# The experts of a transformer stack in steps of 512 hidden channels instead of 256, with the next expert's rows gathered early

## The reference

```python
D_MODEL, SEQ, D_FF_3, N_EXPERTS, TOP_K = 1024, 256, 3584, 8, 2

def swiglu(x, wg, wu, wd):
    return (jax.nn.silu(x @ wg) * (x @ wu)) @ wd

def moe_swiglu(h, w_router, wg, wu, wd):
    xt = h.reshape(-1, d)
    logits = (xt @ w_router).astype(jnp.float32)
    top_v, top_i = lax.top_k(logits, TOP_K)
    gates = jax.nn.softmax(top_v, axis=-1)
    comb = jnp.sum(jax.nn.one_hot(top_i, N_EXPERTS) * gates[..., None], axis=1)
    y = jnp.zeros_like(xt)
    for e in range(N_EXPERTS):
        y = y + comb[:, e:e + 1] * swiglu(xt, wg[e], wu[e], wd[e])
    return y.reshape(bsz, s, d)
```

## Time and profile before

| what | value |
|---|---|
| median of 3 executions | 2552.34 us (2552.05 to 2553.14) |
| profiled execution, its own time | 2553.99 us |
| its span (first to last instruction) | 2552.1 us |
| expert stage: first to last scaling of gathered rows (L1825, 9 times) | 1522.4 to 2532.1 us, 126.2 us per expert |
| PE busy | 2396.1 us, 94% |
| DVE busy | 1965.9 us, 77% |
| ACT busy | 1442.5 us, 57% |
| DMA | 651.79 MB, mean 255 GB/s |

### The profile page before, as it was taken

The page is one execution under the profiler, slowest core; times in us unless marked ns, Lnnn a source line. Parts: engine busy times, 40 slices in busy tenths (PEclk is TensorE's granted clock), DMA queues, the critical chain, the costliest instruction groups (busy, mean ns, idle before and its releaser), DMA issues.

```text
span 2552.1 us, 32705 instructions
## 1 busy us (share of the span) xinstructions
PE 2396.1 (94%) x11965; PEld 2001.3 (78%) x11965; DVE 1965.9 (77%) x1889; ACT 1442.5 (57%) x1418; POOL 17.6 (1%) x33
## 2 busy tenths in 40 slices
PE   4996999998999899799999969999999999999997
PEld 4865788867788798797887968888888888888886
DVE  6888778687687656675445748898989888888897
ACT  2553433546443454464434527777777777777775
POOL 0000000000000000000000000000000000000000
PEclk8997999999999899899999979999999999999998
DMA  8358699534598445455555429999999999999995
GB/s 326 124 173 297 226 317 321 187 121 164 167 329 300 145 163 187 131 170 173 188 183 165 165 83 331 361 340 350 350 340 359 333 366 334 366 334 366 331 368 180
DMA packets 435139, 651.79 MB, mean 255 GB/s; under 512 B 20688, under 2 KB 324432, under 8 KB 435040
## 3 DMA queue, kind: packets, MB, share of 16 engines
q1 hardware_dynamic: 432880, 643.59, 74.0%
q0 software_dynamic: 2160, 6.85, 0.8%
HBM read 649.32 MB, written 1.05 MB: 255 GB/s over the span
## 4 chain that ended last, share of the span: by engine, by line
PE 84%; DVE 9%; ACT 3%; issue 3%; DMA 1%; SPq 0%; DVEq 0%; POOL 0%; ACTq 0%
PE pair L1894 25%; PE pair L1896 25%; PE pair L1895 25%; DVE rest L1079 2%; PE pair L1929 2%; PE tb L2107 2%; DVE aw L1417 1%; ACT head L677 1%; DVE aw L1098 1%; PE pair L2017 1%; PE tb L1972 1%; DMA x<-in_x 1%; ACT aw L706 1%; DVE hT L1200 0%; DVE gat L1825 0%
## 5 line engine op out<-in xcount | busy, mean ns | idle before, releaser
L1079 DVE TENSOR_TENSOR rest<-raw,head 128x2048 fp32r<-128x2048 f32 x546 | 1249.2, 2292 | 296.2 <-ACT head L677 276.4
L677 ACT ACTIVATE head<-raw 128x2048 fp32r<-128x2048 f32 x546 | 1043.2, 1912 | 308.4 <-PE pair L1896 284.9
L1894 PE MATMUL pair<-head,hTh 128*128 128x512 f32 x1864 | 749.4, 402 | 21.2 <-DVE qkv L1509 6.8
L1896 PE MATMUL pair<-head,hTl 128*128 128x512 f32 x1864 | 731.5, 392 | 0.0
L1895 PE MATMUL pair<-rest,hTh 128*128 128x512 f32 x1864 | 730.6, 392 | 0.0
L1894 PEld LDWEIGHTS pair<-head,hTh 128*128 128x128 f32 x1864 | 352.5, 189 | 100.7 <-issue 16.3
L1896 PEld LDWEIGHTS pair<-head,hTl 128*128 128x128 f32 x1864 | 352.0, 189 | 75.0
L1895 PEld LDWEIGHTS pair<-rest,hTh 128*128 128x128 f32 x1864 | 353.0, 189 | 69.3 <-issue 1.5
L1894 PE MATMUL pair<-head,aTh 128*128 128x512 f32 x776 | 307.1, 396 | 2.6 <-issue 2.6
L1895 PE MATMUL pair<-rest,aTh 128*128 128x512 f32 x776 | 303.8, 392 | 0.0
L1896 PE MATMUL pair<-head,aTl 128*128 128x512 f32 x776 | 303.7, 391 | 0.0
(11 more groups left out here) (312 smaller groups left out, 1706.9 us busy)
## 6 DMA issues: line engine op xcount, KB each, us to landing
raw<-in_moe_w_gate SPq DMA_DIRECT2D x224, 512.0 KB, 6.0
raw<-in_moe_w_up SPq DMA_DIRECT2D x224, 512.0 KB, 7.1
raw<-in_moe_w_down SPq DMA_DIRECT2D x224, 512.0 KB, 6.7
raw<-in_w_in SPq DMA_DIRECT2D x152, 512.0 KB, 4.7
raw<-in_ada_w SPq DMA_DIRECT2D x96, 512.0 KB, 5.8
raw<-in_w_ffn_in SPq DMA_DIRECT2D x88, 512.0 KB, 5.5
raw<-in_w_ffn_out SPq DMA_DIRECT2D x44, 512.0 KB, 5.5
raw<-in_w_out SPq DMA_DIRECT2D x40, 512.0 KB, 4.8
```

Of the source, the lines that this page charges most:

```text
L677: act.activation(head[:, c.split, :], raw[:, c.raw, :], ACT.Copy).then_inc(heads_done, 1)
L1079: dve.tensor_tensor(rest[:, c.split, :], raw[:, c.raw, :], head[:, c.split, :].bitcast(F32), ALU.subtract).then_inc(rests_done, 1)
L1894: pe.matmul(out_, lh, rh, start=start, stop=False, skip_group_check=True)
L1896: return pe.matmul(out_, ll, rh, start=False, stop=stop, skip_group_check=True)
```

## The change

An expert's hidden width is taken in 7 steps of 512 channels. The chunks of a step are now six: gate (two halves of the input channels), up (two halves), down (two halves of the 512 hidden channels). A gate or up chunk holds rows of 512 floats of one matrix, where before it held rows of 256 of two. Silu, product and the turned halves work on 512 columns, and the four transposes of a step stand together. Chunk count per expert (42), matmuls and bytes are as before.

At the boundary: the gather for the next expert stands behind step 0 of the present one, `xe` is made there (`gathered_out`), and it is split within the last step (`gathered_head`, `gathered_rest`). TensorE's end of an expert is the last transposes (`turn_wide`), the last down (now two chunks, 24 matmuls, in the order first 512 columns of both, then the second), the next expert's first gate chunk (`first_gate`), and the scatter. The next round then begins at the wait for `weights_ready`. Since `first_gate` does not count its chunk as used, the transposes of `ptok` do. `pslot` has memory of its own. ScalarE and VectorE put the splits of the next expert's first two chunks around `y_head` and `y_rest`.

The dense feed-forwards only lose unused parameters of their helper functions. The diff, cut to the expert part:

```diff
     STEPS3 = F3 // FB
-    PER = 3 * STEPS3
+    EB = 512
+    STEPSE = F3 // EB
+    PER = 6 * STEPSE
...
+        pslot = sb("pslot", [P, T, P], F32R)
...
             def load_expert(it, e):
-                def gu(k, s, r):
-                    cols = slice(s * FB, (s + 1) * FB)
+                def wide(k, w, s, r):
                     c = At(MOE0 + k, it, PER)
-                    load(c.place, c.placed(-RAW), landed[c.raw], [(slice(0, 1024), eg[:, bass.ds(e * KD + 4 * r, 4), cols]),
-                                                                  (slice(1024, 2048), eu[:, bass.ds(e * KD + 4 * r, 4), cols])])
-
-                def dn(k, s):
+                    cols = slice(s * EB, (s + 1) * EB)
+                    load(c.place, c.placed(-RAW), landed[c.raw], [(slice(h * 2 * EB, (h + 1) * 2 * EB), w[:, bass.ds(e * KD + 4 * r + 2 * h, 2), cols])
+                                                                  for h in range(2)])
+
+                def dn(k, s, r):
                     c = At(MOE0 + k, it, PER)
-                    load(c.place, c.placed(-RAW), landed[c.raw], [(slice(0, D), ed[:, bass.ds(e * KF + 2 * s, 1), :]),
-                                                                  (slice(D, 2 * D), ed[:, bass.ds(e * KF + 2 * s + 1, 1), :])])
-                gu(0, 0, 0)
-                gu(1, 0, 1)
-                for s in range(STEPS3 - 1):
-                    gu(2 + 3 * s, s + 1, 0)
-                    gu(3 + 3 * s, s + 1, 1)
-                    dn(4 + 3 * s, s)
-                dn(PER - 1, STEPS3 - 1)
+                    load(c.place, c.placed(-RAW), landed[c.raw], [(slice(h * D, (h + 1) * D), ed[:, bass.ds(e * KF + 4 * s + 2 * r + h, 1), :])
+                                                                  for h in range(2)])
+
+                def gate_and_up(k, s):
+                    wide(k, eg, s, 0)
+                    wide(k + 1, eg, s, 1)
+                    wide(k + 2, eu, s, 0)
+                    wide(k + 3, eu, s, 1)
+
+                def down(k, s):
+                    dn(k, s, 0)
+                    dn(k + 1, s, 1)
+                gate_and_up(0, 0)
+                for s in range(STEPSE - 1):
+                    gate_and_up(4 + 6 * s, s + 1)
+                    down(8 + 6 * s, s)
+                down(PER - 2, STEPSE - 1)
 
...
+            def silu_wide(c, s):
+
+                act.wait_ge(chunk_used, c.count())
+                act.activation(sg_e, EXPERT_BANKS[0][:, 0, :], ACT.Silu).then_inc(sem("silu_ready"), 1)
+
+            def expert_step(c, s):
+
+                make_head(c.next(2))
+                make_head(c.next(3))
+                turned_head(s)
+                make_head(c.next(4))
+                silu_wide(c.next(1), s + 1)
+                for d in (5, 6, 7):
+                    make_head(c.next(d))
...
             def expert(it, window):
-                s0 = it * STEPS3 + STEP0[3]
+                s0 = it * STEPSE + STEP0[3]
                 at = At(MOE0, it, PER)
                 make_head(at.next(2))
-                make_head(at.next(3))
                 act.wait_ge(sem("picks_turned"), it + 1)
                 act.activation(slot_weight, tb[1][:, 256:257], ACT.Copy)
-                act.activation(pslot, tb[1][:, 0:256].rearrange("p (t n) -> p t n", t=T), ACT.Copy).then_inc(sem("slots_ready"), 1)
-                silu_gate(at.next(1), s0, 1, 0, EXPERT_BANKS)
-                for s in range(STEPS3 - 1):
-                    ffn_step(at.next(2 + 3 * s), s0 + s, 1, (s + 1) % 2, EXPERT_BANKS)
-                turned_head(s0 + (STEPS3 - 1), 1)
-                make_head(at.next(PER + 1))
+                act.activation(pslot[:, :, :], tb[1][:, 0:256].rearrange("p (t n) -> p t n", t=T), ACT.Copy).then_inc(sem("slots_ready"), 1)
+                make_head(at.next(3))
+                make_head(at.next(4))
+                silu_wide(at.next(1), s0)
+                make_head(at.next(5))
+                for s in range(STEPSE - 2):
+                    expert_step(at.next(4 + 6 * s), s0 + s)
+                c = at.next(4 + 6 * (STEPSE - 2))
+                make_head(c.next(2))
+                make_head(c.next(3))
+                turned_head(s0 + (STEPSE - 2))
+                make_head(c.next(4))
+                silu_wide(c.next(1), s0 + (STEPSE - 1))
+                make_head(c.next(5))
+                make_head(c.next(6))
+                act.wait_ge(chunk_used, c.next(3).count())
+                gathered_head(it + (window + 2))
+                make_head(c.next(7))
+                turned_head(s0 + (STEPSE - 1))
+                make_head(at.next(PER))
                 act.wait_ge(sem("slots_ready"), it + 1)
                 act.wait_ge(sem("y_half"), it + 1)
                 y_head(0)
-                gathered_head(it + (window + 2))
                 act.wait_ge(chunk_used, at.next(PER - 1).count())
                 y_head(1)
+                make_head(at.next(PER + 1))
...
+
+            def gated_wide(c, s):
+                dve.wait_ge(sem("silu_ready"), s + 1)
+                dve.wait_ge(chunk_used, c.count())
+                dve.tensor_tensor(act_e, sg_e, EXPERT_BANKS[0][:, 1, :], ALU.mult).then_inc(act_ready, 1)
+
+            def expert_step(c, s):
                 make_rest(c.next(2))
-                turned_rest(s, nt)
                 make_rest(c.next(3))
-                gated_hidden(s + 1, nt, b, banks)
+                turned_rest(s)
                 make_rest(c.next(4))
+                make_rest(c.next(5))
+                gated_wide(c.next(3), s + 1)
+                make_rest(c.next(6))
+                make_rest(c.next(7))
...
-            def gathered_rest(count, between=None):
+            def gathered_out(count):
 
                 dve.wait_ge(sem("gather_done"), count)
                 dve.tensor_tensor(xe, pair[2][:, :, :].rearrange("p b (k s) -> p (b k) s", s=P),
                                   over(col8("norm_ffn_3", 1), [P, KD, P], 2), ALU.mult).then_inc(sem("gathered"), 1)
-                if between:
-                    between()
+
+            def gathered_rest(count):
+
                 dve.wait_ge(sem("xe_head"), count)
                 dve.tensor_tensor(hTl[:, :, 0:P], xe, hTh[:, :, 0:P].bitcast(F32), ALU.subtract).then_inc(sem("xe_rest"), 1)
...
             def expert(it, e, window):
-                s0 = it * STEPS3 + STEP0[3]
+                s0 = it * STEPSE + STEP0[3]
                 for t in range(T):
                     ins = dve.tensor_scalar(token_weight[:, t:t + 1], ones[:, 0:1], comb[:, t, bass.ds(e, 1)], None, ALU.mult)
                 ins.then_inc(sem("weights_ready"), 1)
                 dve.wait_ge(sem("picks_turned"), it + 1)
                 pick(lambda c: sm[:, bass.ds(e + (c + 1), 1)])
                 at = At(MOE0, it, PER)
-                make_rest(at.next(2))
-                make_rest(at.next(3))
-                gated_hidden(s0, 1, 0, EXPERT_BANKS)
-                for s in range(STEPS3 - 1):
-                    ffn_step(at.next(2 + 3 * s), s0 + s, 1, (s + 1) % 2, EXPERT_BANKS)
-                turned_rest(s0 + (STEPS3 - 1), 1)
+                for d in (2, 3, 4, 5):
+                    make_rest(at.next(d))
+                gated_wide(at.next(3), s0)
+                for s in range(STEPSE - 2):
+                    expert_step(at.next(4 + 6 * s), s0 + s)
+                    if s == 0:
+                        gathered_out(it + (window + 2))
+                c = at.next(4 + 6 * (STEPSE - 2))
+                make_rest(c.next(2))
+                make_rest(c.next(3))
+                turned_rest(s0 + (STEPSE - 2))
+                make_rest(c.next(4))
+                make_rest(c.next(5))
+                gated_wide(c.next(3), s0 + (STEPSE - 1))
+                make_rest(c.next(6))
+                gathered_rest(it + (window + 2))
+                make_rest(c.next(7))
+                turned_rest(s0 + (STEPSE - 1))
+                make_rest(at.next(PER))
+                y_rest(it, 0)
+                y_rest(it, 1)
                 make_rest(at.next(PER + 1))
-                gathered_rest(it + (window + 2), lambda: y_rest(it, 0))
-                y_rest(it, 1)
                 for t in range(T):
                     dve.wait_ge(sem("scattered"), it * 2 + (t + 1))
                     dve.tensor_tensor(x[:, t, :], x[:, t, :], pair[2 - t][:, :, :].rearrange("p b n -> p (b n)"),
                                       ALU.add).then_inc(sem("scatter_added"), 1)
 
...
+            def wide(c, bank_, r, used=True):
+
+                pe.wait_ge(rests_done, c.placed())
+                for k in range(4):
+                    wcols = slice(k * EB, (k + 1) * EB)
+                    ins = three(bank_, hTh[:, 4 * r + k, 0:P], hTl[:, 4 * r + k, 0:P], head[:, c.split, wcols], rest[:, c.split, wcols],
+                                r == 0 and k == 0, r == 1 and k == 3)
+                if used:
+                    ins.then_inc(chunk_used, 1)
+
...
```

(84 more changed lines are left out.)

83 lines of the change are left out of this document (43 added, 40 removed).

## The result

The changed kernel takes 2607.69 us (median of 4 runs, 2607.07 to 2608.20) against 2552.56 us before on the same chip: a ratio of 1.0216 with a 95% interval of 1.0198 to 1.0233, 55 us slower. From here on "the changed kernel" is this one.

What follows compares the result with a forecast made beforehand. It took PE's instructions plus its boundary waits to bound the expert stage, data being early. Waits of +40.8 us and clock falls of +15 on 2553.99 gave 2609.8, less 1.65 to the median: 2608 us, range 2585 to 2628.

Steps and rivals of the forecast that it cites:

- No gain and no loss inside the steps: Middle of an expert: the tightest rest still ends about 0.7 us early, so no PE wait and no gain.
- Rival 3: Gate and up matmuls run faster with one run of 512 columns; at 30 ns each, 2527 us; chance 0.04.
- Term A: Before the last down: new PE wait of 3.0 us for VectorE's turned_rest, once per expert, +24.0 us.
- Term B: Between scatter and next expert: new wait of 3.3 us for the weights before the picks' transposes, seven boundaries, +23.1 us.
- the small wait before chunk 2: Next expert's start: the existing wait for rest 2 behind the picks, 0.4 to 0.6 us, was said to stay.
- The first turned block: First turn_wide of an expert: the first product comes 0.3 us late, eight times, +2.4 us.
- Term C: Scatter: early gate chunk hides 1.54 us of waits seven times, -10.8 us; additions at the end close later, +2.1 us.
- Term D: Clock: two thirds of the 15 new waits bring a fall to 1.2 GHz, 10 of 1.5 us, +15 us.
- Rival 1: At the boundary: the same waits without clock falls, 2593 us; chance 0.18.
- rival 2: At the boundary: nearly all 15 waits bring a clock fall, some of double length, 2618 to 2638 us; chance 0.15.

Runs made afterwards that it cites:

- experiment 1: Changed kernel with 512-channel steps but the boundary in its old order (gather, row split and next gate chunk put back): 2571.33 us, ratio 1.0076.
- the fast version: Changed kernel with the reordered boundary queues and late additions of experiment 5, plus the gather put back before the last down: 2544.78 us, ratio 0.9971.
- Experiment 2: Changed kernel with only the gather and the split of its rows put back between the last transposes and the last down: 2574.22 us, ratio 1.0088.
- Experiment 3: Changed kernel with only the next expert's weight columns written earlier, before the second y_rest: 2588.67 us, ratio 1.014.
- experiment 5: Changed kernel, gather still early, with ScalarE's and VectorE's boundary queues reordered and the additions to x moved into the next round: 2572.42 us, ratio 1.0081.
- experiment 4: Changed kernel with 24 useless matmuls of 256 columns behind each scatter, where PE would wait for the weights: 2591.20 us, ratio 1.0152.
- experiment 7: Changed kernel with 16 useless matmuls of 256 columns (1.83 us) behind each expert's gather: 2628.14 us, ratio 1.0305.

## Why the prediction was right

The forecast was 2608, the median is 2607.7. The two waits and the falls of the clock were there, with the releasers I had named. That the number fits to 0.3 us is luck: the waits were taken 5 us too long and the clock 4.6 us too short.

**No gain and no loss inside the steps** held: a step takes 16.81 us where two took 2 x 8.41, experiment 1 has no PE wait there, and the fast version with the same steps keeps PE busy for 99% of the stage. Rival 3, a shorter slot for gate and up, is out: from 1653.61 to 1656.33 the twelve gate matmuls take 2.72 us, 0.227 each, as the down matmuls do.

**Term A** (last down, 3.0 us, 24 in all) was there with the queue I named: 2.55 us idle in the trace, and 2.8 by the distance of matmul starts (the fourth transpose at 1645.21, the down at 1648.04, where inside a step it is 0.03), 22.4 in all. The 512-wide prices (0.58 and 0.68 measured) lay within my bounds of 0.38 to 0.68 and 0.42 to 0.75. Experiment 2 removed it by putting the gather back.

**Term B** (weights, 3.3 us, 23.1) was there: 1657.91 + 0.23 = 1658.14 to 1661.19, 3.05 us, 21.4 in all. Experiment 3 showed what I had named as late next, `rest` 2, and experiment 5 that all of it can leave PE's path. I had one thing wrong: the small wait before chunk 2 doesn't stay. The chunk in front of it runs at the lower clock and PE comes later (its last matmul starts at 1667.22, the next chunk's first at 1667.63, a slot of the lower clock and no wait). The 2.8 us of a long fall have that gain in them.

**The first turned block** (0.3 us) has 0.9 us of idle weight load; in experiment 4, in rounds where the clock holds, 0.4. PE itself loses less: in experiment 2, behind the first boundary, where the clock held, the last matmul starts at 1668.84 and the transposes at 1669.18, 0.34 us for a slot of 0.23. That is 0.1 us, 0.8 in all; what more there is behind a fall is in the price of the fall.

**Term C** (scatter, -10.8, end +2.1): no wait is left in the scatter, and the additions close 1658.54 + 2.34 - 1653.61 = 7.3 us behind the last down (7.5 forecast).

**Term D** (clock, 10 falls of 1.5 us, 15 in all) had the right mechanism and nearly the right sum, but the count and the length of a fall were off: 7 falls, all behind the wait for the weights and none behind the last down, each 6.8 us long and worth 2.8, 19.6 us. PE's busy time grew by 17 us beyond the 2.7 of the chunk too many, of the same size as this. Experiment 4 gives 16.5 us directly, with three short falls left over. The fault was to take a mean over 15 waits when the falls depend on more than length. Rival 1 (no falls) is out with experiment 4; rival 2 (nearly all 15 waits bring one) is out by count, 7 of 15.

With the measured terms the sum is 22.4 + 21.4 + 0.8 - 10.8 + 1.8 + 19.6 = 55.2, against 55.1 measured. Terms A, B and the first turned block were each taken some 1.6 us too long and the falls of the clock 4.6 us too short.

The Trainium skill (TensorE: Matmul & The Clock Gate, "HAM oscillation") describes a kernel in which a wait for data of some 3 to 5 us in every tile makes each next tile start at the lower clock. The trace of the changed kernel agrees for its waits of 2.9 us, shorter than those, seven of seven. It differs for the waits of 2.55 us there, none of eight, and experiment 2 differs for the same 2.9 us, five of seven.

What stays open is what decides whether a wait brings a fall, and of which length. The runs show that it isn't the length of the wait alone. The clock records of the changed kernel and of experiments 1 to 5 and 7 show one regularity: each of the 13 long falls starts 0.4 to 0.9 us before its wait ends, while 27 of the 29 short ones start only after it, by 0.1 to 1.8 us (the other two start 0.5 and 0.6 us before the end of a wait of 2.6 us). In the changed kernel the rounds of 133.2 us and the falls 133.12 us apart keep step, so each wait meets the same case; in experiment 2 the rounds are 127.5 to 130.3 us and the case changes. That is read from the traces and was not tested apart.

## What to carry to other kernels

Before an operation is moved out of a place, look at what it hides there: the gather was 3.5 us of work that gave ScalarE and VectorE the time to split the last block, and moving it away cost 22.4 us, more than the 10.8 of the scatter's waits that the rest of the change removed. Count a boundary as a chain across all engines from the last common event, with everything queued ahead of each step, and compare it with PE's cover; a chunk that covers one wait has been taken from another. Then bring the short operations that others wait for (here two columns of 0.33 us) ahead of the long ones that nobody waits for yet, and a boundary of 3 us waits becomes one of some 0.5 us, with the early chunk as a gain. Follow the last round to the end as well: work that is only useful ahead of a next round stands there without one.

## What the runs showed of the hardware

A PE wait can cost more than its length. The same wait of 2.9 us brought no fall of the clock, one of 3.4 us or one of 6.8 us, priced at 0, 1.6 and 2.8 us (all three in experiment 2); waits of 2.55 us brought none in the changed kernel and seven short falls at eight waits in experiment 7, with 1.8 us of work more in the round. The long falls began while PE still waited, nearly all short ones after it had started again. Filling the wait for the weights with useless matmuls made the changed kernel 16.5 us faster (experiment 4).

Loads of gate and up, now in rows of 2 KB in place of 1 KB, landed sooner (median 4.5 and 4.7 us from issue, 6.0 and 7.1 before). So did the loads of down, whose rows are as before (4.2 us, 6.7 before), so the row length is not shown to be the cause for each load by itself. The time did not notice, since `raw` buffers, not transfers, were what SyncE waited for.
